# Expert weights loaded in the order of their use, the tail's copies and branch ahead of its choices, and two pairs' gate/up weights in halves

## The chip, the core and the metric

The kernel runs on one core of a Trainium2 chip. Its time is the device time of one execution in microseconds. The core has TensorE (matmuls, PE in the profile), VectorE (DVE), ScalarE (ACT), GpSimd (POOL) and SyncE (SP), each with its own queue of instructions that run in order; they wait for each other by semaphores. Sixteen DMA engines move data between HBM and the on-chip memory; in this kernel SyncE issues nearly all weight loads, GpSimd the gathers and scatters of rows.

## What is computed

One decoder layer on 512 rows of 1024 numbers in float32: a modulated norm, a mixer of gated linear attention and sparse softmax attention, an output projection, and then a mixture of 32 experts. The part that the change touches is the last:

```python
hg = jnp.einsum('td,edf->tef', ht, w_g)
hu = jnp.einsum('td,edf->tef', ht, w_u)
act = jax.nn.silu(hg) * hu * combine[..., None].astype(hg.dtype)
y = jnp.einsum('tef,efd->td', act, w_d)
...
y = hier_moe(h, ...)
x = x + gate_f * rmsnorm(y, g_post_ffn[l])
```

`combine` is nonzero for two experts of each row, the two choices. Each expert has a gate and an up matrix of 1024 x 256 and a down matrix of 256 x 1024.

## The kernel before

**Experts in pairs.** The 32 experts are worked off as 16 pairs (`NPAIR`), each expert with 64 places for rows. Pair j goes through: a gather of its 128 rows (GpSimd, L1226), their transposition (TensorE `turn_rows`, L870), the gate/up product (`gate_up_product`, L883, 32 matmuls into bank G or S0), silu and product (ScalarE L1624, VectorE L2278), a transposition of the result (`turn_act`, L900), the down product (`down_product`, L912, 16 matmuls into banks A0 and A1), two copies to `yb` (`y_left` on VectorE, L2288; `y_right` on ScalarE, L1638), and a scatter of the rows to `y_dram` (GpSimd, L1231). Pair 15 has no scatter; its rows stay in `yb` and are added at the end.

**TensorE's order.** Up to pair 13 (`OWN_DOWN`) the down product of pair j-1 follows the gate/up product of pair j; from pair 13 on a pair's own down product follows too. So the order of use of the weights is gate/up(1), down(0), gate/up(2), down(1), ..., gate/up(13), down(12), down(13), gate/up(14), down(14), gate/up(15), down(15).

**Weight loads.** A pair has 4 MB of gate/up weights (four loads of 1 MB) and 2 MB of down weights (two loads), in three sets of buffers, so pair j's loads go to set j % 3. SyncE issues them by `experts` (L1031), for pair j first the wait for the gate/up product of pair j-3 and its four loads, then the wait for the down product of pair j-3 and its two loads. Only pair 15 is different (L1065 to L1074): its gate/up weights come as eight loads of half the rows' length, and TensorE waits for the second halves (`we_last`) in the middle of the product.

**Tail.** When all scatters are stored (`y_stored`), SyncE loads `y_dram` in four tiles of 128 rows with both choices (`y_load`, L1080, into `yc`, 1 MB each). ScalarE scales the first choice (`first_choice`, L1668), VectorE adds the scaled second one (`both_choices`, L2321). TensorE multiplies pair 15's rows with a matrix that places and weights them (`last_hot`, L958); for tiles 0 and 1 VectorE adds that product (`add_last`, L2341), for tiles 2 and 3 TensorE adds the choices itself through an identity matmul (L954). Then come the sum of squares (ScalarE L1691, L1696), `root`, `scaled` (L2347, L2351), a square root (ScalarE L1698), `final` (L2365) and the output. ScalarE and VectorE have the first two choices ahead of their copies of pair 15. A branch on `n_ov`, the number of extra pairs for experts with more than 64 rows, stands in every engine's queue; the traced execution takes it with 0 extra pairs.

## Time and profile before

| | us |
|---|---|
| median of 3 runs | 798.15 |
| lowest and highest run | 796.47, 798.77 |
| profiled execution | 795.45 |
| its span, first to last instruction | 793.6 |
| TensorE busy in the span | 702.3 |
| VectorE busy in the span | 411.6 |
| ScalarE busy in the span | 287.9 |

Times of the trace are counted from the start of the span. The pairs begin at about 529 us and end at about 766 us; the rest of the span is the tail. A view of stretches gives busy times in a window; a timeline gives single instructions; the chain of waits is followed back from the last instruction, at each step to what released it, and "issue" in it is time in which an engine waited for nothing that the profile can name, as a load whose semaphore it does not resolve.

### The profile page before, as it was taken

How to read it: one execution, taken by the hardware profiler on the slowest of the kernel's cores; microseconds unless marked ns; L12 is line 12 of the kernel's file. 1: busy time of each engine (PE TensorE's matmuls, PEld its weight loads, DVE VectorE, ACT ScalarE, POOL GpSimd, SP SyncE). 2: the span in 40 equal slices, each digit the busy share in tenths (PEclk: the TensorE clock that was granted, in tenths of full speed). 3: DMA queues.
4: the chain of work that ended last, by engine and by line, in shares of the span. 5: the costliest groups of instructions: out<-in, count | busy, mean ns of one | idle time of the engine just before them, and what ended most of it. 6: DMA issues, size and time to landing. Idle time of an engine off the chain costs nothing.

```text
span 793.6 us, 9709 instructions
## 1 busy us (share of the span) xinstructions
PE 702.3 (88%) x3447; PEld 445.4 (56%) x3447; DVE 411.6 (52%) x876; ACT 287.9 (36%) x512; POOL 120.9 (15%) x148
## 2 busy tenths in 40 slices
PE   1899989898999999999999799989889868788974
PEld 0447747566776777777777688763333323333321
DVE  2386958998897666644312735654351211112128
ACT  5133254254447778532232225342121211111224
POOL 3064852210002112000000001010122111111000
PEclk9999999999997999999999999999989998999998
DMA  9989730411311030303355162798999999999962
GB/s 343 388 302 369 285 136 1 115 57 50 107 46 61 2 106 2 107 0 107 107 212 185 60 234 79 293 407 322 416 417 420 419 422 419 419 419 421 403 272 106
DMA packets 49724, 179.27 MB, mean 226 GB/s; under 512 B 9560, under 2 KB 13762, under 8 KB 35340
## 3 DMA queue, kind: packets, MB, share of 16 engines
q1 hardware_dynamic: 43732, 166.26, 53.7%
q0 software_dynamic: 4784, 8.19, 2.9%
q10 hardware_dynamic: 1160, 4.20, 1.4%
q8 instruction: 28, 0.46, 0.2%
q14 instruction: 20, 0.16, 0.1%
HBM read 174.13 MB, written 12.59 MB: 235 GB/s over the span
## 4 chain that ended last, share of the span: by engine, by line
PE 53%; DVE 17%; DMA 8%; issue 7%; ACT 4%; DVEq 0%; POOL 0%; ACTq 0%; SPq 0%; POOLq 0%; PEldq 0%
PE psA L479 9%; PE psA L481 8%; PE psA L480 8%; PE psS L883 6%; PE psA L912 6%; PE psG L883 5%; DVE mk_mem L1833 3%; DVE m L1832 3%; DMA y_dram<-sig_mem,tables 2%; DMA arena<-y_dram 1%; PE psT L870 1%; DVE arena_r L1781 1%; DMA xn_dram<-sig_mem 1%; DMA arena<-in_w_out_dram 1%; DMA kv<-xn_dram,tables 1%
## 5 line engine op out<-in xcount | busy, mean ns | idle before, releaser
L479 PE MATMUL psA<-arena_r 128*128 128x512 f32 x320 | 130.1, 406 | 4.7 <-DVE arena_r L1781 4.1
L480 PE MATMUL psA<-arena_r 128*128 128x512 f32 x320 | 125.9, 393 | 0.0
L481 PE MATMUL psA<-arena_r 128*128 128x512 f32 x320 | 125.8, 393 | 0.0
L1781 DVE TENSOR_TENSOR arena_r<-arena,arena_r 128x1024 fp32r<-128x1024 f32 (+1 forms) x37 | 60.5, 1657 | 38.5 <-ACT arena_r L1305 37.6
L479 PEld LDWEIGHTS psA<-arena_r 128*128 128x128 f32 x320 | 60.9, 190 | 25.6 <-issue 13.7
L883 PE MATMUL psS<-arena,kv 128*64 128x512 f32 x224 | 64.6, 664 | 11.1 <-issue 10.9
L481 PEld LDWEIGHTS psA<-arena_r 128*128 128x128 f32 x320 | 60.7, 190 | 13.4
L480 PEld LDWEIGHTS psA<-arena_r 128*128 128x128 f32 x320 | 61.0, 191 | 12.0 <-issue 0.2
L883 PE MATMUL psG<-arena,kv 128*64 128x512 f32 x208 | 58.2, 611 | 4.8 <-issue 4.8
L1305 ACT CAST arena_r<-arena 128x1024 fp32r<-128x1024 f32 (+1 forms) x31 | 49.8, 1629 | 20.7 <-DMA arena<-in_w_in_dram 10.1
L2278 DVE TENSOR_TENSOR sig_mem<-sig_mem,psS 128x256 f32<-128x256 f32 x8 | 4.9, 613 | 81.7 <-ACT sig_mem L1624 81.7
L883 PEld LDWEIGHTS psS<-arena,kv 128*64 128x64 f32 x224 | 21.7, 151 | 41.8 <-issue 41.3
L1231 POOL DMA_INDIRECT y_dram<-sig_mem,tables x16 | 15.9, 993 | 182.8 <-issue 115.1
L479 PE MATMUL psA<-arena_r,qs_mem_r 128*128 128x512 f32 x96 | 38.9, 405 | 4.3 <-DVEq L2024 3.5
L912 PE MATMUL psA<-qs_mem,sig_mem 128*64 128x512 f32 x80 | 39.2, 633 | 4.0 <-ACT sig_mem L1629 4.0
L2278 DVE TENSOR_TENSOR sig_mem<-sig_mem,psG 128x256 f32<-128x256 f32 x8 | 4.9, 612 | 65.6 <-ACT sig_mem L1624 65.6
L883 PEld LDWEIGHTS psG<-arena,kv 128*64 128x64 f32 x208 | 19.1, 140 | 28.2 <-issue 27.3
L480 PE MATMUL psA<-arena_r,qs_mem_r 128*128 128x512 f32 x80 | 31.7, 397 | 0.0
L471 PE MATMUL psA<-arena,kv 128*128 128x512 f32 x64 | 29.4, 623 | 1.8 <-DMA arena<-in_w_in_dram 1.8
L1450 ACT ACTIVATE qs_mem<-qs_mem,sm 128x128 f32<-128x128 f32 (+3 forms) x32 | 17.9, 560 | 29.5 <-DVE sm L1969 28.4
L1638 ACT COPY sig_mem<-psA 128x512 f32<-128x512 f32 x16 | 9.3, 584 | 52.0 <-PE psA L912 27.6
L1832 DVE MAX8 m<-mk_mem 128x8 f32<-128x256 f32 (+2 forms) x48 | 26.9, 560 | 2.2
(440 smaller groups left out, 1293.2 us busy)
## 6 DMA issues: line engine op xcount, KB each, us to landing
arena<-in_w_e_gate_dram SPq DMA_DIRECT2D x25, 1024.0 KB
arena<-in_w_e_up_dram SPq DMA_DIRECT2D x25, 1024.0 KB
arena<-in_w_in_dram SPq DMA_DIRECT2D x11, 2048.0 KB, 8.3
arena<-in_w_e_down_dram SPq DMA_DIRECT2D x12, 1024.0 KB, 15.6
qs_mem<-in_w_e_down_dram SPq DMA_DIRECT2D x10, 1024.0 KB, 19.7
arena<-in_w_ada_dram SPq DMA_DIRECT2D x4, 2048.0 KB, 17.1
qT<-in_w_ada_dram SPq DMA_DIRECT2D x6, 1024.0 KB, 5.4
gvs<-in_w_ada_dram SPq DMA_DIRECT2D x5, 1024.0 KB, 6.2
```

Of the source, the lines that this page charges most:

```text
L471: last = nc.tensor.matmul(a[:, :], hT[:, k, tt * P:(tt + 1) * P], w[:, k, :], start=(k == 0), stop=(k == KD - 1))
L479: nc.tensor.matmul(acc, lhs[0], rhs[0], start=start, stop=False)
L480: nc.tensor.matmul(acc, lhs[0], rhs[1], start=False, stop=False)
L481: return nc.tensor.matmul(acc, lhs[1], rhs[0], start=False, stop=stop)
L883: last = nc.tensor.matmul(ps[g][64 * q:64 * q + 64, :].rearrange("p (g f) -> p g f", g=2), h2g[:, b, k, 64 * q:64 * q + 64], gu, start=(k ...
L912: last = nc.tensor.matmul(ps[name][64 * q:64 * q + 64, :], actT[:, b, kf, 64 * q:64 * q + 64], down_sets[z][q][:, D * kf + 512 * n:D * kf ...
L1231: pool.indirect_dma_start(out=y_dram, out_offset=bass.IndirectOffsetOnAxis(ap=column, axis=0), in_=yb[:, b, :], in_offset=None, bounds_che ...
L1305: nc.scalar.copy(hi[:, part], src[:, part]).then_inc(hi_ready, 4 if q is None else 1)
L1450: nc.scalar.activation(prob[:, u % 2, hh, 0:n], prob[:, u % 2, hh, 0:n], ACT.Exp, bias=sm[:, hh, z:z + 1], scale=-1.0, accum_out=sm[:, hh, ...
L1781: V.tensor_tensor(lo[:, part], src[:, part], hi[:, part], ALU.subtract).then_inc(lo_ready, 4 if q is None else 1)
L1832: step(V.max(m8[:, :], work))
L1833: step(V.match_replace(work, m8[:, :], work, TAKEN))
```

## The change

It does five things.

- The issue order of the loads. Gate/up of pair 2 stands ahead of down of pair 1. From pair 3 on SyncE issues gate/up of pair j+1 and then down of pair j, for j from 3 to 12, and then down of pair 13. The waits are the same as before, load by load.
- The gate/up weights of pair 14 are loaded in halves too, as pair 15's; TensorE has a semaphore for each of the two pairs.
- On ScalarE and VectorE the copies of pair 15 and the branch come first, and all four choices behind them. The square root's table load and a first small root stand between branch and choices. SyncE reads the branch's number ahead of the y loads and issues these once.
- TensorE starts every tile's sum with pair 15's rows and adds the choices by an identity matmul for tiles 1, 2 and 3 (before: 2 and 3); VectorE adds only for tile 0. The order of VectorE's tail follows.
- Three small loads at the start share one semaphore; the wait for two of them is now for all three.

```diff
-            pe.wait_ge(ld_small, 32)
+            pe.wait_ge(ld_small, 48)
...
-                    pe.wait_ge(ld_a2, 16)
+                    pe.wait_ge(ld_small, 48)
...
-            def gate_up_product(j, b, z, loads, g, g_turn, last_pair=False):
+            def gate_up_product(j, b, z, loads, g, g_turn, half_pair=None):
...
-                    if last_pair and k == KD // 2:
-                        pe.wait_ge(we_last, 16 * 4)
+                    if half_pair is not None and k == KD // 2:
+                        pe.wait_ge(we_last[half_pair], 16 * 4)
...
-                pe.wait_ge(fss_ready, 4)
-
-            pe.wait_ge(yb_ready, NPAIR)
-            for tt in range(TT):
-                if tt >= 2:
-                    pe.wait_ge(sum_ready, (1, 3)[tt - 2])
+
+            def last_part(tt):
+
                 for half, (name, turns) in enumerate(sum_banks[tt]):
                     if name == "S1":
                         take("S1", "sum")
                     else:
-                        pe.wait_ge(bank[name].free, base[name] + turns)
-                    if tt >= 2:
-                        nc.tensor.matmul(ps[name][:, :], ident[:, :], yc[:, tt, 0, 512 * half:512 * (half + 1)], start=True, stop=False)
-                for half, (name, turns) in enumerate(sum_banks[tt]):
+                        pe.wait_ge(bank[name].free, base[name] + turns + (0 if name == "S0" else n_ov))
                     if half:
                         pe.wait_ge(yb_act, NPAIR)
-                    last = nc.tensor.matmul(ps[name][:, :], last_hot[:, tt, :], yb[:, 1, 512 * half:512 * (half + 1)], start=(tt < 2), stop=True)
+                    last = nc.tensor.matmul(ps[name][:, :], last_hot[:, tt, :], yb[:, 1, 512 * half:512 * (half + 1)], start=True, stop=(tt == 0))
+                if tt == 0:
+                    last.then_inc(sum_full, 1)
+
+            def other_part(tt):
+
+                pe.wait_ge(fss_ready, tt + 1)
+                for half, (name, _) in enumerate(sum_banks[tt]):
+                    last = nc.tensor.matmul(ps[name][:, :], ident[:, :], yc[:, tt, 0, 512 * half:512 * (half + 1)], start=False, stop=True)
                 last.then_inc(sum_full, 1)
+
+            pe.wait_ge(yb_ready, NPAIR)
+            for tt in range(3):
+                last_part(tt)
+            other_part(1)
+            last_part(3)
+            other_part(2)
+            other_part(3)
...
             sp.wait_ge(ring_out, len(items))
+            gate_up(2, 0, 4)
+            gate_up(2, 1, 5)
             down(1, 0, 2)
             down(1, 1, 3)
-            gate_up(2, 0, 4)
-            gate_up(2, 1, 5)
...
-            for j in range(3, NPAIR - 1):
-
-                experts(j % 3, 2 * j, 2 * j + 1, MOE_G[(j - 3) % 2], (j - 3) // 2 + 1, j - 2)
-            j, z = NPAIR - 1, (NPAIR - 1) % 3
...
+            pair_gate_up(3)
+            for j in range(3, OWN_DOWN):
+                pair_gate_up(j + 1)
+                pair_down(j)
+            pair_down(OWN_DOWN)
+            for j in range(NPAIR - 2, NPAIR):
+                z = j % 3
...
+                for half in range(2):
+                    part = slice(1024 * half, 1024 * (half + 1))
...
+                pair_down(j)
...
-            for b in range(2):
-                sp.wait_ge(y_stored[b], 16 * (NPAIR // 2))
-            y_load()
             sp.wait_ge(slot_ready, 2)
             n_ov = sp.value_load(ovi[0:1, NOV:NOV + 1], min_val=0, max_val=NOV // 2)
...
+            sp.wait_ge(y_stored[1], 16 * (NPAIR // 2))
+            sp.wait_ge(y_stored[0], 16 * (NPAIR // 2 + n_ov))
+            for tt in range(TT):
+                sp.dma_start(yc[:, tt, :, :], y_v[tt]).then_inc(yc_in[tt], 16)
...
-            first_choice(0, 1, fw_ready)
-            first_choice(1, 1, fw_ready)
             y_right(NPAIR - 1, 1, NPAIR // 2)
...
+            nc.scalar.activation(st[:, 44:45], st[:, 34:35], ACT.Sqrt)
+            first_choice(0)
+            first_choice(1)
+            square(0)
+            first_choice(2)
+            rooted(0)
+            first_choice(3)
+            for tt in range(1, TT):
+                square(tt)
+                rooted(tt)
...
-            both_choices(0, (fw_ready, 1), fss_ready)
             y_left(NPAIR - 1, 1, NPAIR // 2)
-            both_choices(1, (fw_ready, 2), fss_ready)
...
-            both_choices(2, (fw_late, 1), sum_ready)
+            both_choices(0)
             add_last(0)
+            both_choices(1)
             scaled(0)
-            both_choices(3, (fw_late, 2), sum_ready)
+            both_choices(2)
             root(0)
-            add_last(1)
-            scaled(1)
-            root(1)
             final(0)
-            final(1)
-            root(2)
-            scaled(2)
-            final(2)
-            root(3)
-            scaled(3)
-            final(3)
+            both_choices(3)
+            for tt in range(1, TT):
+                root(tt)
+                scaled(tt)
+                final(tt)
```

SyncE's queue, before, from the gate/up loads of pair 3 on (`arena` with gate and up: pair 3; then down of pair 3; then gate/up of pair 4):

```order
L1021 DMA arena<-in_w_e_gate_dram 128x2048
L1021 DMA arena<-in_w_e_up_dram 128x2048
L1029 DMA arena<-in_w_e_down_dram 128x2048 [waits A1_full]
L1029 DMA arena<-in_w_e_down_dram 128x2048
L1021 DMA arena<-in_w_e_gate_dram 128x2048 [waits S0_full]
L1021 DMA arena<-in_w_e_up_dram 128x2048
```

And in the changed kernel, the same place:

```order
L1032 DMA arena<-in_w_e_gate_dram 128x2048
L1032 DMA arena<-in_w_e_up_dram 128x2048
L1032 DMA arena<-in_w_e_gate_dram 128x2048 [waits S0_full]
L1032 DMA arena<-in_w_e_up_dram 128x2048
L1032 DMA arena<-in_w_e_gate_dram 128x2048
L1032 DMA arena<-in_w_e_up_dram 128x2048
L1040 DMA arena<-in_w_e_down_dram 128x2048 [waits A1_full]
L1040 DMA arena<-in_w_e_down_dram 128x2048
```

The four loads of pair 4, with their wait on S0 (pair 1's gate/up product), moved ahead of the two down loads of pair 3 with their wait on A1 (pair 0's down product).

ScalarE's queue at the end, before, from pair 15's second transposition copy to the first square; `yc_in0` to `yc_in3` are the y tiles (the body of the loop over extra pairs, which the rows contain in part, is not run):

```order
L1629 COPY sig_mem<-psO 128x256 [waits O_full]
L1668 ACTIVATE arena<-arena,rtmp_mem 128x1024 [waits actT_ready,yc_in0]
L1668 ACTIVATE arena<-arena,rtmp_mem 128x1024 [waits yc_in1]
L1638 COPY sig_mem<-psA1 128x512 [waits y_stored1,A1_full]
L1673 COMPARE_AND_BRANCH [waits yb_act]
```

```order
L1673 UNCONDITIONAL_BRANCH [waits yc_in3,yc_in2]
L1668 ACTIVATE arena<-arena,rtmp_mem 128x1024 [waits yc_in2]
L1668 ACTIVATE arena<-arena,rtmp_mem 128x1024 [waits yc_in3]
L1687 ACT_TABLE_LOAD
L1687 ACTIVATE st<-st 128x1
L1691 ACTIVATE qs_mem,st<-arena 128x1024 [waits sum_ready]
```

And in the changed kernel:

```order
L1637 COPY sig_mem<-psO 128x256 [waits O_full]
L1646 COPY sig_mem<-psA1 128x512 [waits actT_ready,y_stored1,A1_full]
L1673 COMPARE_AND_BRANCH [waits yb_act]
```

```order
L1673 UNCONDITIONAL_BRANCH
L1702 ACT_TABLE_LOAD
L1702 ACTIVATE st<-st 128x1
L1684 ACTIVATE arena<-arena,rtmp_mem 128x1024 [waits yc_in0]
L1684 ACTIVATE arena<-arena,rtmp_mem 128x1024 [waits yc_in1]
L1690 ACTIVATE qs_mem,st<-arena 128x1024 [waits sum_ready]
L1684 ACTIVATE arena<-arena,rtmp_mem 128x1024 [waits yc_in2]
```

The copy from A1 moved from behind two choices to ahead of all; the table load moved from behind the fourth choice to ahead of the first.

## Rows read from the trace of the kernel before

**Rows 1.** Stretches: us; busy us (count) PE PEld DVE ACT POOL; clock, DMA share, GB/s.

```profile
550.50:552.00 1.50, 1.50 (x10) 0.43 (x6) 1.22 (x6) 0.00 (x0) 0.00 (x0) 1.00 0.00 0
...
732.00:748.00 16.00, 15.05 (x70) 4.89 (x70) 2.75 (x6) 3.31 (x8) 1.96 (x2) 1.00 1.01 412
...
552.00:620.00 68.00, 62.42 (x300) 23.82 (x296) 26.36 (x68) 13.93 (x35) 11.16 (x11) 0.95 1.01 412
620.00:750.00 130.00, 105.90 (x470) 40.77 (x470) 21.12 (x48) 22.33 (x55) 16.13 (x16) 0.92 1.02 419
...
722.00:726.00 4.00, 3.98 (x12) 1.47 (x14) 0.00 (x0) 0.00 (x0) 0.61 (x1) 0.63 1.01 421
```

**Rows 2.** Chain of waits, pairs 2 to 13: start, us, what.

```profile
578.07 6.13 PE psA L912 x16
...
620.01 3.00 issue
623.01 8.78 PE psS L883 x32
...
636.62 2.54 issue
639.16 7.09 PE psG L883 x32
...
718.83 3.19 issue
722.02 8.78 PE psS L883 x32
...
732.05 3.58 PE psA L912 x16
```

**Rows 3.** TensorE's timeline, gate/up of pairs 14 and 15, down of 15.

```profile
740.66 0.59 PE L883 MATMUL psG<-gvs,kv 128*64 128x512 f32 x1
...
753.20 7.04 PE L883 MATMUL psS<-arena,kv 128*64 128x512 f32 x32
...
762.25 3.65 PE L912 MATMUL psA<-arena,sig_mem 128*64 128x512 f32 x16 [0.46 <-ACT sig_mem L1629]
```

**Rows 4.** SyncE's timeline, the loads down(3) and gate/up(4).

```profile
551.42 0.80 SPq L1029 DMA_DIRECT2D arena<-in_w_e_down_dram  x2
552.27 0.43 SPq L1021 DMA_DIRECT2D arena<-in_w_e_gate_dram  x1
```

**Rows 5.** TensorE's timeline, the operation after pair 1's gate/up product.

```profile
546.49 0.44 PE L900 MATMUL psO<-ident,sig_mem 128*128 128x128 f32 x2
```

**Rows 6.** SyncE's last weight issues, then DMA issues with us to landing.

```profile
736.31 2.13 SPq L1071 DMA_DIRECT2D arena<-in_w_e_up_dram  x1
738.49 3.76 SPq L1029 DMA_DIRECT2D arena<-in_w_e_down_dram  x2
arena<-in_w_e_up_dram SPq DMA_DIRECT2D x1, 512.0 KB, 18.6
arena<-in_w_e_down_dram SPq DMA_DIRECT2D x1, 1024.0 KB, 19.6
```

**Rows 7.** Chain of waits, the store of pair 14's rows.

```profile
754.83 6.32 DMA y_dram<-sig_mem,tables
```

**Rows 8.** ScalarE's timeline, the last choice and the table load.

```profile
774.63 1.15 ACT L1668 ACTIVATE arena<-arena,rtmp_mem 128x1024 f32<-128x1024 f32 x1 [1.33 <-DMA arena<-y_dram]
775.80 1.28 ACT L1687 ACT_TABLE_LOAD   x1
777.09 0.20 ACT L1687 ACTIVATE st<-st 128x1 f32<-128x1 f32 x1
```

**Rows 9.** VectorE's timeline, the copy of pair 15 and the last two finals.

```profile
769.41 0.69 DVE L2288 COPY sig_mem<-psA 128x512 f32<-128x512 f32 x1
...
786.25 1.28 DVE L2365 SCALAR_TENSOR_TENSOR qT<-arena,st,qT 128x1024 f32<-128x1024 f32 x1
...
789.36 1.41 DVE L2365 SCALAR_TENSOR_TENSOR qT<-arena,st,qT 128x512 f32<-128x512 f32 x2
```

More of the change, by code:

```diff
@@ L1087, in _ @@
             with sp.If(n_ov > 0):
-                sp.wait_ge(fss_ready, 2)
-                for tt in (2, 3):
-                    sp.wait_ge(yc_in[tt], 16)
                 with sp.Fori(0, n_ov) as v:
@@ L1663, in _ @@
                     act_taken(j, j % 2)
-            def first_choice(tt, loads, done):
-                act.wait_ge(yc_in[tt], 16 * loads)
-                nc.scalar.activation(yc[:, tt, 0, :], yc[:, tt, 0, :], ACT.Copy, scale=rt[:, 9, tt:tt + 1]).then_inc(done, 1)
-            first_choice(0, 1, fw_ready)
-            first_choice(1, 1, fw_ready)
             y_right(NPAIR - 1, 1, NPAIR // 2)
@@ new lines, in first_choice, with square @@
+            def first_choice(tt):
+                act.wait_ge(yc_in[tt], 16)
+                nc.scalar.activation(yc[:, tt, 0, :], yc[:, tt, 0, :], ACT.Copy, scale=rt[:, 9, tt:tt + 1]).then_inc(fw_ready, 1)
+            def square(tt):
+                if tt == 0:
+                    act.wait_ge(sum_ready, 1)
+                    nc.scalar.activation(scratch2, yc[:, tt, 0, :], ACT.Square, accum_out=st[:, tt:tt + 1]).then_inc(fms_ready, 1)
+                    return
+                act.wait_ge(sum_full, tt + 1)
+                for half, (name, _) in enumerate(sum_banks[tt]):
+                    n = tt + 20 * half
+                    nc.scalar.activation(scratch2[:, 512 * half:512 * (half + 1)], ps[name][:, :], ACT.Square, accum_out=st[:, n:n + 1]).then_inc(fms_ready, 1)
@@ L2330, in _, with both_choices @@
                     y_left(NPAIR + v, 0, NPAIR // 2 + v)
-                for tt in range(2):
-                    both_choices(tt, (fw_ready, tt + 3), fss_ready)
-                dve.wait_ge(fss_ready, 4)
-            dve.wait_ge(fss_ready, 2)
+            def both_choices(tt):
+                y = yc[:, tt, :, :]
+                dve.wait_ge(fw_ready, tt + 1)
+                V.scalar_tensor_tensor(y[:, 0, :], y[:, 1, :], rt[:, 10, tt:tt + 1], y[:, 0, :], ALU.mult, ALU.add).then_inc(fss_ready, 1)
             def add_last(tt):
+                dve.wait_ge(fss_ready, tt + 1)
                 dve.wait_ge(sum_full, tt + 1)
@@ L2353, in root @@
             def root(tt):
[L2355 to L2356 removed]
+                dve.wait_ge(fms_ready, 2 * tt + 1)
+                if tt:
                     step(V.tensor_tensor(st[:, tt:tt + 1], st[:, tt:tt + 1], st[:, 20 + tt:21 + tt], ALU.add))
```

69 lines of the change are left out of this document (22 added, 47 removed).

## The prediction

> **What bounds the kernel now.** I read the execution by stretches first. From 620 to 750 us the DMA engines are busy at a share of 1.02 while TensorE is busy for 106 of 130 us [rows 1]: the expert weights set the pace. Then I read the chain of waits [rows 2]. In each pair TensorE computes gate/up (L883), turns rows, computes the down product of the pair before (L912), and waits: 3.00 us ahead of pair 7's gate/up, 2.54 ahead of pair 8's, and so on, seven times, the last 3.19 ahead of pair 13's. Those are weights landing; gate/up products are then 16.5 us apart ((722.02 - 623.01) / 6). From 722.02 on the chain is work and handoffs only: pair 14's gate/up starts at 740.66, 18.6 us later, pair 15's at 753.20, another 12.5 us later, and its down product ends at 765.9 (762.25 + 3.65) [rows 3]. So the end is set by when pair 13's gate/up weights land and then by the tail: store of pair 14's rows, loads of y, sums, output.
>
> **Part 1, the order of the weight loads.** Before, SyncE issues down(j), then gate/up(j+1), each behind a wait for its buffers. From pair 3 on the new order is gate/up(j+1), then down(j), up to down(12); from down(13) on everything keeps its place in the stream, since down(13) stood ahead of gate/up(14) already. Two effects.
>
> (a) A hole. Pair 4's gate/up goes out at 552.27, behind down(3), which waited until 551.42 for a down product [rows 4]. Its own condition, the end of pair 1's gate/up, was fulfilled at 546.5, when TensorE's next operation starts [rows 5]. In the new order it goes out there, while the engines are still busy. From 550.5 to 552 no engine moves anything, and from 552 to 620 none rests (share 1.01) [rows 1]. So every later landing gains between 1.5 us (the stretch in which even the slowest engine was idle) and 4.7 us (551.4 - 546.7). A weight has landed when its slowest engine is done, so I go near the lower end: **2.2 us**.
>
> (b) Position. Gate/up(j+1) no longer has the 2 MB of down(j) ahead of it, a third of a pair's 6 MB: it lands 16.5 / 3 = 5.5 us earlier, for pairs 4 to 13. Pair 13's lands at 722.0 - 5.5 - 2.2 = 714.3. Down(12) lands 5.5 us behind it, at 719.8. Its product starts 10.0 us after gate/up(13) (732.05 - 722.02 [rows 2]), at 724.3, so 4.5 us of cover remain for the load that was moved back.
>
> From 714.3 TensorE keeps its distances: gate/up(14) at 732.9, gate/up(15) at 745.5. Are their weights there? The last piece of pair 15's gate/up lands at 754.9 (736.31 + 18.6), the last down piece at 760.2 (about 740.6, the second issue of the pair of rows at 738.49, + 19.6) [rows 6]. Between 722.0 and 754.9 lie down(13), gate/up(14), down(14) and gate/up(15), 12 MB, so 2.7 us per MB. With 2.2 us taken off: gate/up(14) first half 730.8, second 736.3; gate/up(15) first half 747.2, second 752.7; last down 758.0.
>
> **Part 2, halves for pair 14.** Whole, gate/up(14) would wait until 736.3; in halves its first half runs from 732.9 to 736.4: worth 3.4 us there, of which little is left behind it, because gate/up(15) waits for its own weights in either case. SyncE issues eight transfers instead of four; with the ring full an issue takes as long as the drain (2.13 us for 512 KB [rows 6]), so the split itself is hidden. Does a 512 KB transfer cost more per byte? While pair 15's halves run (732 to 748) the stream moves 412 GB/s, against 419 over the stage [rows 1]. The last down piece, a whole 1 MB, lands 5.3 us behind the last half piece: this slow rate at the end belongs to the slowest engine and not to the size. I take nothing; the ends are 0 and 5.3 - 2.7 = 2.6 us per MB.
>
> The Trainium skill (DMA: Bandwidth & Descriptors, section Bandwidth) speaks against halves: it asks for at least 1 MiB per DMA, and its section Anatomy of one DMA fits about 2 us of fixed cost to each. By that, four more transfers would cost up to 8 us of stream; the 412 GB/s say that in a full queue the fixed part overlaps.
>
> **The end of the products.** Gate/up(15) starts with its first half at 747.2, is through it at 750.7 (half of 7.0 [rows 3]), waits until 752.7 and needs 3.5 us more at the full clock. But gate/up took 8.78 us after waits of 3.0 us and more, with a granted clock of 0.63 in its first 4 us, against 7.09 after a wait of 2.54 [rows 1, 2]; here two waits of 1.7 and 2.0 us come close together. I add 1.7. End: 757.9 instead of 760.2. Down(15) starts 2.0 us later as before (762.25 against 753.20 + 7.04), at 759.9, behind its weights (758.0), and ends at **763.5, 2.4 us earlier**. That, and not 7.7, is what remains of part 1: the 5.5 us of position end with pair 13, since the last bytes keep their place.
>
> **Part 3, the tail.** Before, pair 14's rows are issued at 754.83 and stored 6.3 us later [rows 7]; then y is loaded, and the last of its four tiles is used at 774.63 [rows 8]. VectorE has its copy of pair 15 done only at 770.1 (769.41 + 0.69) [rows 9], though the product ended at 765.9: the first two choices stood ahead of it. After: the store goes out 7.7 us earlier, at 747.1, beside full traffic; with 6.3 to 11 us it ends before or at 758.0, when the weights do. The four loads queue behind those: 4 MB at 412 GB/s, the last lands at about 768.5.
>
> ScalarE: copy of pair 15 done at 764.5 (0.3 + 0.7); the branch, not seen alone, between 0 and 0.7 us, the nearest being the 0.7 between VectorE's copy end and its next choice, which contains a wait: I take 0.2. The table load and the small root (1.28 + 0.20), which stood at 775.80 behind all choices [rows 8], now stand ahead of them: 766.2. The first choice takes 1.15 [rows 8]. VectorE starts at 767.4. An operation over 1024 columns takes 1.28 us, one in two halves 1.41 [rows 9]: choice(0) 1.28, add_last(0) 1.41, choice(1), scaled(0), choice(2) 3.84, root 0.15, final(0) 1.43 with its reciprocal, choice(3) 1.28: 776.8, and 0.2 for waits on ScalarE, whose squares and choices fit between. Then three tiles at 3.1 us (789.36 - 786.25 [rows 9]), the last only to its first half: 777.0 + 3.1 + 3.1 + 2.5 = **785.7, against 790.1** (789.36 + 0.75). TensorE's identity products of tiles 1 to 3 have a choice each as cover. The small load that now shares a semaphore stands directly behind the two others; nothing.
>
> The Trainium skill (ScalarE: Activation LUTs, section What ACT_TABLE_LOAD costs) puts about 1.38 us of drain beside a load of 1.28. The row agrees in the 1.28, but the next operation starts 0.01 us behind the load [rows 8]. By the Trainium skill the gain would be up to 1.4 us smaller.
>
> **Sum.** 2.4 us by the products, 2.0 by the tail's order (24.2 us from product to last final become 22.2): 4.4. Span 793.6 - 4.4 = 789.2, profiled execution 795.45 - 4.4 = 791.1. That execution is 2.7 us under the median of the runs (798.15), so I forecast 793.7.
>
> **Rivals.** *More (0.17):* the stream gains 3.5 us or more, or the clock stays up through the short waits of gate/up(15), as it did after 2.54 us. Then down(15) ends near 761: 6 to 8 us in all, 791.3. *Only the tail (0.18):* the slowest engine gains nothing from the hole, or the stores of pairs 13 and 14 now take their share inside the stream; down(15) stays near 765.5. 796.0, at the edge of what can be told. *Nothing (0.09):* the waits inside gate/up(15) leave TensorE at 1.2 GHz to the end: its second half takes 7.0 instead of 3.5 us and down(15) 6.1 as at 578.07 [rows 2], so it ends at 767.9 and the tail's 2.0 pays for it: 798. Against it: in the chain a slow gate/up is followed by a down product of 3.58 us. *Slower (0.05):* halves cost. At the 5.3 us per MB of the last piece, pair 14's 4 MB land 10.4 us later, with all that follows: 804. Half that price, 5.2 us, gives 799; it decides from 4.4 us on, where the gain is used up. Against it: the 412 GB/s. By the rule of the Trainium skill on DMA size, 8 us, it would be 801.7.
>
> **Chances.** About 0.3% (2.4 us) is what a measurement can tell from no change. Forecast 0.51, all faster; More 0.17, faster; Only the tail 0.18, half of it faster; Nothing 0.09; Slower 0.05, of which 0.01 within the bound. Faster 0.77, same 0.19, slower 0.04. The range goes down to 789.5, into More, and up to 797.3, across Only the tail and the near side of Nothing.
>
> **What would show it.** Right: pair 4's gate/up issued at about 547 and no hole behind it; gate/up(7) without a wait; gate/up(13) at about 714; pair 15's copies ahead of all choices; the last final near 785.7. Wrong: gate/up(13) at 719 or later (a), down products waiting for their weights (b), halves of pair 14 landing more than 3 us per MB apart (part 2), a y tile landing after 772 or a pause around the table load (part 3).

## The result, and the profile after

The changed kernel takes 790.91 us, median of six runs (788.68 to 791.67). The kernel before, beside it, took 795.61 (793.08 to 798.77, six runs; the 798.15 that I started from was the median of three of these). The ratio of the two is 0.9916, 95% interval [0.9895, 0.9937]: 6.7 us (5.0 to 8.4) gained where I had forecast 4.4. The two medians as they stand differ by less, 4.7 us: the six runs of before lie in two groups, 796.5 to 798.8 and 793.1 to 794.8. I go by the ratio, since the same kernel timed again (after_again, below) gives 0.9918 with medians of 790.37 and 797.04, 6.7 us apart.

The profiled execution took 791.03 us with a span of 789.2, which is the predicted span to the tenth. That agreement is an accident, as the next paragraphs show.

Stretches of after (us; busy us and count of PE, PEld, DVE, ACT, POOL; granted clock, DMA share, GB/s), then SyncE's timeline there:

```profile
549.00:552.00 3.00, 3.00 (x20) 1.67 (x21) 2.24 (x6) 2.18 (x6) 0.00 (x0) 1.00 0.99 370
552.00:620.00 68.00, 63.25 (x306) 24.26 (x302) 27.65 (x74) 13.95 (x35) 11.17 (x11) 0.95 1.01 419
620.00:750.00 130.00, 108.45 (x498) 41.01 (x496) 22.78 (x50) 24.21 (x59) 17.10 (x17) 0.95 1.02 417
```

```profile
548.93 0.33 SPq L1032 DMA_DIRECT2D arena<-in_w_e_gate_dram  x1
...
553.77 0.81 SPq L1040 DMA_DIRECT2D arena<-in_w_e_down_dram  x2
```

Against [rows 1]: where no engine moved anything in the last 1.5 us before 552, the share is now 0.99. Pair 4's gate/up is issued at 548.93 (546.8 when its stage is set to start with that of before), ahead of down(3), and not at 552.27 behind it [rows 4]. The stage as a whole moves 419 and 417 GB/s in the two long stretches, where before moved 412, with the hole at its start, and 419.

TensorE's timeline of after at gate/up(7), gate/up(13), both halves of gate/up(15), and down(15) (start, us, what, number of matmuls, idle time before it and what ended it; of the products of pairs 7 and 13 only the first few matmuls stand in the row):

```profile
621.69 1.89 PE L884 MATMUL psS<-arena,kv 128*64 128x512 f32 x8
...
715.75 1.08 PE L884 MATMUL psS<-arena,kv 128*64 128x512 f32 x4 [2.05 <-issue]
...
749.07 3.65 PE L884 MATMUL psS<-arena,kv 128*64 128x512 f32 x16 [1.45 <-issue]
754.46 3.65 PE L884 MATMUL psS<-arena,kv 128*64 128x512 f32 x16 [1.74 <-DMA arena<-in_w_e_up_dram]
759.22 0.44 PE L901 MATMUL psO<-ident,sig_mem 128*128 128x128 f32 x2 [1.11 <-DVE sig_mem L2291]
760.21 3.65 PE L913 MATMUL psA<-arena,sig_mem 128*64 128x512 f32 x16 [0.56 <-ACT sig_mem L1637]
```

Gate/up(7) starts without the 3.00 us of wait of [rows 2]. Pair 15 is bound by its weights: the second half starts as they land, after 1.74 us.

**A common zero.** The expert stage does not start at the same time in each execution. The first gate/up product (pair 0's) starts at 529.55 in the profile of before and at 531.71 in that of after, 2.2 us later, and the one edit ahead of it does not explain this (behind the small loads with the shared semaphore, SyncE issues a load of `w_in` at 173.98 us before and 173.67 after, so they are not it). In the profiles of the kernels below it lies between 527.9 and 538.0. A good part of this goes with TensorE's granted clock far ahead of the stage: from 250 to 300 us it is 0.86 in four of the fourteen profiles, this one of after among them, and 0.93 to 0.97 in the ten others, before with 0.95. A copy of GpSimd that starts at 300.10 in before starts at 303.9 to 305.6 in those four and at 298.4 to 303.6 in the others. What makes the clock differ there no run shows. So all times of the stage are from here on counted from that product's start. In these terms the product of down(15) ends at 236.35 before (765.9 - 529.55) and 232.15 after (763.86 - 531.71), **4.2 us earlier, and not 2.4**. From there to the start of the last final it takes 23.46 us before and 21.48 after (785.34 - 763.86): **2.0 less, as forecast**. The way from there to the end of the span is 0.4 shorter (4.24 and 3.86). Sum 6.6, well inside the ratio's 5.0 to 8.4; the span shows only 4.4 of it because its stage began 2.2 late.

The tail as the chain of waits of after has it (start, us, what):

```profile
735.79 18.53 DMA arena<-in_w_e_up_dram
754.46 3.67 PE psS L884 x16
760.21 3.67 PE psA L913 x16
765.08 1.28 ACT L1702
766.58 1.05 ACT arena L1684
767.65 1.30 DVE arena L2340
...
785.34 0.75 DVE qT L2372
```

The store of pair 14 [rows 7] and the loads of y (10.04 us from 762.09 in the chain of before) are gone from it; the last piece of pair 15's gate/up weights (issued 735.79, landed 754.3), both products, then ScalarE's table load and first choice set the end.

### The profile page after: what moved, and what is told of

The parts are those of the page before. It is cut to its first block, busy times and chain, and to the rows that moved or that the text cites. A ratio compares the mean times of both kernels' runs of the same rounds, so it can differ in the third digit from the quotient of the medians.

```text
span 789.2 us, 9728 instructions
## 1 busy us (share of the span) xinstructions
PE 703.0 (89%) x3451; PEld 447.0 (57%) x3451; DVE 411.7 (52%) x876; ACT 287.7 (36%) x514; POOL 120.9 (15%) x148
## 4 chain that ended last, share of the span: by engine, by line
PE 48%; SPq 13%; DVE 13%; DMA 8%; ACT 4%; issue 3%; POOL 0%; DVEq 0%; ACTq 0%; POOLq 0%; PEldq 0%
PE psA L480 10%; PE psA L482 10%; PE psA L481 10%; SPq L1032 5%; SPq L1090 4%; SPq L1040 4%; PE psS L884 3%; PE psA L913 3%; DMA arena<-in_w_e_up_dram 2%; PE psG L884 2%; DVE mk_mem L1846 2%; DMA y_dram<-sig_mem,tables 2%; DVE m L1845 2%; PE psO L611 1%; PE psT L598 1%
## 5 line engine op out<-in xcount | busy, mean ns | idle before, releaser
L480 PEld LDWEIGHTS psA<-arena_r 128*128 128x128 f32 x320 | 61.5, 192 | 24.4 <-issue 12.3
L482 PEld LDWEIGHTS psA<-arena_r 128*128 128x128 f32 x320 | 61.5, 192 | 13.5
L481 PEld LDWEIGHTS psA<-arena_r 128*128 128x128 f32 x320 | 61.5, 192 | 12.2 <-issue 0.2
L884 PE MATMUL psG<-arena,kv 128*64 128x512 f32 x208 | 61.2, 642 | 7.6 <-issue 7.6
L884 PE MATMUL psS<-arena,kv 128*64 128x512 f32 x224 | 58.5, 611 | 9.8 <-issue 7.9
L884 PEld LDWEIGHTS psS<-arena,kv 128*64 128x64 f32 x224 | 20.1, 140 | 37.4 <-issue 36.9
L1411 ACT ACTIVATE sig_mem<-psA 128x512 f32<-128x512 f32 x16 | 9.6, 598 | 50.8 <-PE psA L482 50.8
```

The lines of the kernel that those rows point to most:

```text
L480: nc.tensor.matmul(acc, lhs[0], rhs[0], start=start, stop=False)
L481: nc.tensor.matmul(acc, lhs[0], rhs[1], start=False, stop=False)
L482: return nc.tensor.matmul(acc, lhs[1], rhs[0], start=False, stop=stop)
L884: last = nc.tensor.matmul(ps[g][64 * q:64 * q + 64, :].rearrange("p (g f) -> p g f", g=2), h2g[:, b, k, 64 * q:64 * q + 64], gu, start=(k ...
```

## The experiments

Each kernel was timed against the kernel before in the same rounds on the same chip, in several sets of rounds on several chips. All ratios are to before, with 95% intervals; they are not quotients of the medians, from which they differ by 0.1% at most, and by 0.25% for the changed kernel. "gate/up(13)" and "product end" count from pair 0's gate/up; tail is from product end to the start of the last final. The three come from the timelines of one profiled execution of each kernel, the ratio from 6 to 12.

| kernel | ratio, interval | gate/up(13) | product end | tail |
|---|---|---|---|---|
| before | 1 | 192.5 | 236.35 | 23.46 |
| changed kernel | 0.9916 [0.9895, 0.9937] | 184.0 | 232.15 | 21.48 |
| after_again | 0.9918 [0.9881, 0.9955] | 183.4 | 231.76 | 21.45 |
| order_only | 0.9954 [0.9933, 0.9975] | 183.3 | 232.44 | 23.26 |
| tail_only | 0.997 [0.9954, 0.9986] | 193.2 | 236.70 | 21.46 |
| whole14 | 0.9912 [0.9885, 0.994] | 183.6 | 233.06 | 21.47 |
| hole_only | 0.9963 [0.9944, 0.9981] | 189.2 | 233.06 | 23.43 |
| place_only | 0.9999 [0.9978, 1.002] | 187.4 | 235.27 | 24.02 |
| early_table | 0.9894 [0.9873, 0.9915] | 183.2 | 231.38 | 20.09 |
| halves_all | 0.9987 [0.9969, 1.0006] | 188.0 | 236.41 | 21.48 |
| thirds_table | 0.9907 [0.9887, 0.9927] | 183.1 | 234.38 | 20.08 |
| thirds_filled | 0.9929 [0.9905, 0.9954] | 183.8 | 234.47 | 20.08 |
| early_filled | 0.9915 [0.9889, 0.994] | 183.7 | 233.56 | 20.08 |
| thirds_fill2 | 0.992 [0.9893, 0.9947] | 183.7 | 232.05 | 20.06 |

### The change taken apart: order, tail, halves

**order_only** is the kernel before with only the new order of the loads; **tail_only** is the changed kernel with the old order of the loads and with pair 14's gate/up weights whole. The loads in tail_only, against the changed kernel:

```diff
+            down(1, 0, 2)
+            down(1, 1, 3)
             gate_up(2, 0, 4)
             gate_up(2, 1, 5)
-            down(1, 0, 2)
-            down(1, 1, 3)
...
-            pair_gate_up(3)
-            for j in range(3, OWN_DOWN):
-                pair_gate_up(j + 1)
+            for j in range(3, NPAIR - 1):
+                pair_gate_up(j)
                 pair_down(j)
-            pair_down(OWN_DOWN)
-            for j in range(NPAIR - 2, NPAIR):
+            for j in range(NPAIR - 1, NPAIR):
```

> The kernel before with the new order of the loads alone: gate/up(j+1) ahead of down(j), pair 2's gate/up ahead of pair 1's down. Pair 14's gate/up whole, the tail as before. Theory (landings): relative to the start of the pairs, pair 13's gate/up starts 7 to 9 us earlier, pair 15's gate/up ends about 4.3 us earlier (its second half still lands last) and its down product too. The tail's old order then works with y tiles that land some 6 us earlier, so 4 to 6 us in all, ratio 0.993 to 0.995. Rival (the tail carries the gain, the stream is bound by its bytes): pair 15's down product ends within 1 us of before, ratio 0.998 to 1.000.

> The changed kernel with the old order of the loads and pair 14 whole: only the tail is new. Theory: from the end of pair 15's down product to the last final 22.2 us instead of 24.2, all products where they were, 2.0 to 2.3 us in all, ratio 0.997 to 0.998. Rival (the tail's order is worth the greater part of the measured 6.7 us): 20 us or less from product to last final, ratio 0.993 or below.

Order alone gives 3.7 us (1 - 0.9954, of 796.7), tail alone 2.4; 0.9954 x 0.997 = 0.9924, against 0.9916 for the whole. At the product end order_only gains 3.9 us where I had 2.4 for this part, and tail_only nothing (236.70); tail_only's tail is 2.0 shorter, order_only's 0.2. order_only's 0.9954 falls just short of the 0.993 to 0.995 that I had expected for it, with 4.3 us expected at the product end.

**whole14** is the changed kernel with pair 14's gate/up weights in whole loads again:

```diff
-            for j in range(NPAIR - 2, NPAIR):
+            pair_gate_up(NPAIR - 2)
+            pair_down(NPAIR - 2)
+            for j in range(NPAIR - 1, NPAIR):
```

> The changed kernel with pair 14's gate/up loaded whole; pair 15 in halves as in both. Theory (halves of pair 14 are not on the path that ends last): gate/up(14) starts about 3 us later, gate/up(15) up to 2 us later, but its second half's landing still decides: its end and the time as in the changed kernel within 0.5 us, ratio to before 0.991 to 0.993. Rival 1 (halves are worth what they cover, 3.4 us): about 3 us slower than the changed kernel, ratio 0.995 to 0.997. Rival 2 (small transfers cost stream time): faster than the changed kernel by 2 us or more, ratio below 0.990.

0.9912 against 0.9916: halves of pair 14 are worth nothing that can be seen in time, either way. Its product end of 233.06 in the profile, 0.9 us behind the changed kernel's where at most 0.5 was expected, has another cause, of which below. The last piece of pair 15 comes earlier here: the second half of gate/up(15), which waits for it, starts at 221.7 from the start of pair 0's gate/up, against 222.75 in the changed kernel, 222.45 in after_again and 222.07 in early_table, which have pair 14 in halves.

### Hole and position apart

**hole_only**: the old order, except that gate/up(4) goes ahead of down(3). **place_only**: the new order from down(4) on, except that gate/up(4) stays behind down(3).

First hole_only against the old order, written out in the names of the changed kernel, then place_only against the new one (both keep the tail, pair 14 and the gate/up(2) of before):

```diff
             pair_gate_up(3)
+            pair_gate_up(4)
             pair_down(3)
-            pair_gate_up(4)
             pair_down(4)
```

```diff
             pair_gate_up(3)
-            for j in range(3, OWN_DOWN):
+            pair_down(3)
+            pair_gate_up(4)
+            for j in range(4, OWN_DOWN):
                 pair_gate_up(j + 1)
                 pair_down(j)
```

> The kernel before with a single move: pair 4's gate/up loads ahead of pair 3's down loads; every later load keeps its place. Theory: no stretch without DMA between 547 and 553 (relative to the start as before), every later landing 2.2 us earlier (between 1.5 and 3.5), pair 15's second half lands about 2.2 us earlier, product and tail move with it: 1.8 to 2.5 us, ratio 0.997. Rival (the slowest engine gains nothing from the hole, landings stay): ratio 0.999 to 1.001, pair 13's gate/up within 0.5 us of before.

> The kernel before with the loads of gate/up(j+1) ahead of down(j) from j = 4 on, while down(3) stays ahead of gate/up(4), so that the hole at 550.5 to 552 us stays; tail and pair 14 as before. All times here count from the start of pair 0's gate/up product. Theory (position and hole are two separate gains): pair 13's gate/up starts about 5.5 us earlier than the 192.5 of before, at 186 to 187.5, but the last half piece of pair 15 lands where it did (225.4), so the product end is set by weights at 235.4 to 236.0 against 236.35, and the time is within 0.1% of before (794.8 to 795.6 where before is 795.6). Rival (position is what pays at the end too): of the 3.9 us that the whole new order gained at the product end, position carries half or more; then the product end is at 234.4 or earlier and the time 793.6 or less, ratio 0.9975 or less.

The hole is most of it: 2.9 of the 3.7 us in time, more than the 1.8 to 2.5 expected, and 3.3 at the product end. Its size could have been read from the trace of before: the DMA share there is 0.12 from 549 to 550.5 us, 0.00 to 552 and 0.76 to 554, which makes 3.3 us of rest for the mean engine, against 0.35 in hole_only (0.89, 0.88 and 1.02). The position by itself moves gate/up(13) 5.1 us forward (192.5 - 187.4; 5.5 forecast), but its product end only 1.1, and the tail gives half of that back (24.02 against 23.46); in time nothing. That is the step of the forecast that the 5.5 us of position end with pair 13, and it holds. Neither kernel moves the loads of pair 2: at gate/up(13) hole and position give 3.3 + 5.1 = 8.4 us and order_only 9.2; what that move is worth by itself was not tested. Pair 15's second half in place_only, by TensorE's timeline:

```profile
750.92 3.60 PE L883 MATMUL psS<-arena,kv 128*64 128x512 f32 x16
755.27 3.65 PE L883 MATMUL psS<-arena,kv 128*64 128x512 f32 x16 [0.75 <-DMA arena<-in_w_e_up_dram]
```

755.27 - 529.76 (its first gate/up) = 225.5. Before, the last half piece landed at 225.4 (754.9 - 529.55): same bytes ahead, same landing. In the changed kernel it lands at 222.6 (754.3 - 531.7), so the stream gained 2.7 us, of which place_only shows that the position is not the cause.

### The size of the pieces

**halves_all** gives the gate/up weights of pairs 3 to 13 the same halves as pairs 14 and 15:

```diff
             def pair_gate_up(j):
-                next_gate_up(j % 3, 2 * j, 2 * j + 1, MOE_G[(j - 3) % 2], (j - 3) // 2 + 1)
+                z, g = j % 3, MOE_G[(j - 3) % 2]
+                sp.wait_ge(bank[g].full, moe_base[g] + (j - 3) // 2 + 1)
+                for half in range(2):
+                    part = slice(1024 * half, 1024 * (half + 1))
...
+                            sp.dma_start(gu_sets[z][q][:, 2048 * n:2048 * (n + 1)][:, part], src[2 * j + q][:, part]).then_inc(we_in[z], 16)
```

> The changed kernel with the gate/up weights of pairs 3 to 13 in pieces of 512 KB as well: 44 more transfers in the stream, same bytes, same order. Theory (in a full queue a transfer has no fixed price): the stream keeps its 417 GB/s within 1%, landings and time stay within 0.5 us (790.4 to 791.4 where the changed kernel has 790.9). Rival (each transfer has a fixed price that isn't hidden): the smallest price that could be seen, 0.05 us each, gives 2.2 us; by the Trainium skill, DMA: Bandwidth & Descriptors, which asks for at least 1 MiB per DMA and has about 2 us of fixed cost for each, 44 of them would cost up to 88 us.

The theory falls. Product end is 4.3 us later than in the changed kernel, and the ratio goes from 0.9916 to 0.9987. The DMA engines' summary from 552 to 750 us, first after, then halves_all:

```profile
DMA packets 15385, 82.69 MB, mean 418 GB/s; under 512 B 3453, under 2 KB 3453, under 8 KB 7144
```

```profile
DMA packets 20910, 81.71 MB, mean 413 GB/s; under 512 B 4069, under 2 KB 4069, under 8 KB 17819
```

And the stretches (columns as above), one of after and then those of halves_all:

```profile
540.00:550.00 10.00, 9.28 (x50) 4.58 (x50) 1.99 (x5) 2.44 (x7) 0.99 (x1) 1.00 0.96 394
```

```profile
540.00:550.00 10.00, 8.92 (x47) 4.32 (x48) 1.96 (x6) 2.84 (x8) 0.99 (x1) 1.00 0.96 303
552.00:620.00 68.00, 65.39 (x316) 25.24 (x314) 28.62 (x75) 14.59 (x37) 11.20 (x11) 0.97 1.03 413
620.00:750.00 130.00, 105.40 (x470) 39.85 (x468) 21.39 (x48) 22.66 (x57) 16.16 (x16) 0.91 1.02 412
```

The engines are no less busy (share 1.02 and 1.03), but move 0.98 MB less in the window, 2.3 us of stream, with 5,500 packets more: the shorter rows come as more and smaller packets. Another 0.9 MB (2.2 us) is missing from 540 to 550, where after moves 394 GB/s and halves_all 303. Together that is, within 0.2, the 4.3 us, or 0.1 us on average for each of the 44 transfers more. The starts of the products that wait for their weights agree: gate/up(9), with 28 transfers more ahead of it, comes 2.5 us later than in the changed kernel, gate/up(13), with all 44, 4.0. Whether the price is one per transfer or one per packet this experiment does not tell, since both rose together. My reason for costing halves at nothing, that 412 GB/s is close to 419, overlooked that a difference of this size matters once it holds for the whole stage. For pair 14 alone, four transfers, it is by this average 0.4 us, which whole14 could not resolve in time. The Trainium skill (DMA: Bandwidth & Descriptors, section Bandwidth) has the right sign with its advice of at least 1 MiB per DMA; the 2 us of fixed cost of its section Anatomy of one DMA would make 88 us of 44 transfers (an estimate from a figure that the page fits to single transfers issued by GpSimd; those here are issued by SyncE into a full queue), and the trace shows a twentieth of that.

### The table load

**early_table** moves the small root, and with it the table load, to ahead of ScalarE's copy of pair 15:

```diff
+            nc.scalar.activation(st[:, 44:45], st[:, 34:35], ACT.Sqrt)
             y_right(NPAIR - 1, 1, NPAIR // 2)
...
-            nc.scalar.activation(st[:, 44:45], st[:, 34:35], ACT.Sqrt)
             first_choice(0)
```

> The changed kernel with the load of the table for the root moved once more: from behind pair 15's copy (765.08 us, 1.28 us) to ahead of it, where ScalarE waits 3.84 us for pair 15's down product. Theory (with the order of the changed kernel, ScalarE's chain copy, branch, table, first choice sets the tail): the first choice starts 1.5 us earlier (1.28 of load, 0.20 of small root), VectorE's first combined choice too, and all behind it; tail from product end to last final 21.5 - 1.5 = 20.0, time 0.9981 of the changed kernel's, 789.4 where that has 790.9. Rival (VectorE or the loads of y set the tail, or loading the table holds the queue longer than its row shows): 0.5 us or less, tail 21.0 or more.

ScalarE's timeline of early_table:

```profile
758.00 0.37 ACT L1637 COPY sig_mem<-psO 128x256 f32<-128x256 f32 x1 [1.16 <-PE psO L901]
758.48 1.28 ACT L1672 ACT_TABLE_LOAD   x1
759.77 0.20 ACT L1672 ACTIVATE st<-st 128x1 f32<-128x1 f32 x1
762.13 0.58 ACT L1646 COPY sig_mem<-psA 128x512 f32<-128x512 f32 x1 [2.15 <-PE psA L913]
763.32 2.19 ACT L1686 ACTIVATE arena<-arena,rtmp_mem 128x1024 f32<-128x1024 f32 x2 [0.61 <-ACT sig_mem L1646]
```

The load now lies in a wait, and 2.15 us of that wait are left. The tail is 1.4 us shorter, in this profile (20.09) and in the four more that have the edit (20.06 to 20.08; without it 21.45 to 21.48 in five). That is the load of 1.28 and 0.1 for the small root, not 1.5. It gives the lowest time of the study, 788.24 us, ratio 0.9894, near what was expected (0.9981 of the changed kernel's time, with a tail of 20.0); the interval still overlaps that of the changed kernel. The Trainium skill (ScalarE: Activation LUTs, section What ACT_TABLE_LOAD costs) has about 1.38 us of drain beside the load; here the next operation starts 0.01 us behind it, and taking the load off the path brings 1.4 us and not 2.7.

### The clock at the end of the products

My sum had 1.7 us for a clock lost across the two short waits of gate/up(15). In the changed kernel it was not lost, and in none of the nine profiles of kernels with the new order and the new tail does gate/up(15) run at the lower clock, whatever its waits. Stretches of after, the wait for the second half and the second half:

```profile
752.60:754.40 1.80, 0.12 (x2) 0.00 (x0) 0.00 (x0) 0.00 (x0) 0.00 (x0) 1.00 0.76 316
754.40:758.20 3.80, 3.65 (x16) 1.27 (x16) 0.00 (x0) 0.05 (x1) 0.00 (x0) 1.00 0.34 142
```

To see whether it can be, four kernels move the wait or fill it. **thirds_table** is early_table with pair 15's second half in two quarters, the last one waited for with two of eight steps left. **thirds_filled** is thirds_table with five products more ahead of down(15), whose results nothing uses, **thirds_fill2** the same with two. **early_filled** is early_table with four of them ahead of gate/up(15)'s second half. The first two cuts are of thirds_table, the last two of thirds_filled:

```diff
+                    if half_pair == 1 and k == 6:
+                        pe.wait_ge(we_last[2], 16 * 4)
...
-                for half in range(2):
+                for half, part in enumerate((slice(0, 1024), slice(1024, 2048)) if j == NPAIR - 2 else (slice(0, 1024), slice(1024, 1536), slice(1536, 2048))):
...
+            def fill(n):
+                pe.wait_ge(bank["T0"].free, base["T0"] + NPAIR)
+                for i in range(n):
+                    nc.tensor.matmul(ps["T0"][:, :], ident[:, :], h2g[:, 1, 0:4, :], start=True, stop=True)
...
                     turn_act(j, j % 2)
+                    if j == NPAIR - 1:
+                        fill(5)
```

> The early table load together with a third piece in pair 15: its gate/up rows come as one half and two quarters, and the product waits for the last quarter with two of its eight steps left instead of four. Counted from the start of pair 0's gate/up. Theory (the last piece of gate/up sets the product end): it lands where the second half landed (222.6), behind it lie 1.8 us of gate/up instead of 3.6, but the last down weights land at 227.5 and down(15) started at 228.5, so at most 1.0 us is to be had: product end 231.2 to 231.6 instead of 232.15, tail 20.0, sum 2.1 to 2.5 us under the changed kernel: 788.6 where that has 790.9, ratio to before 0.989. Rivals: the quarters add nothing to the early table (789.4), since pair 15's first half or the rows it multiplies come too late for it; or smaller pieces land later and it is slower than the early table alone.

> The kernel of thirds_table with five products more (identity by pair 15's rows, 512 columns, into a free bank, results unused) between the turn of pair 15's activations and its down product, where TensorE waited 2.62 us for weights and then ran at a granted clock of 0.50 (6.39 us instead of 3.65). Theory (the waits around the last product can cost the clock, the mechanism of my added 1.7 us, which only did not strike in the profile of the changed kernel): kept busy, TensorE runs down(15) in 3.65 to 3.8 us, product end 231.4 to 231.9 from the start of pair 0's gate/up instead of 234.38, and the time comes down to that of early_table or 1 us under it: ratio 0.988 to 0.989. Rival (the clock fell for another reason): down(15) stays at 5 us or more, ratio stays at 0.9907. Second rival: the fill delays the product itself, start of down(15) later than 228.4.

> The kernel of early_table with four such products ahead of the second half of pair 15's gate/up, where TensorE waited 1.88 us and kept its full clock. Theory (that wait alone does not cost the clock in most executions): product end 231.3 to 231.8, time as early_table within 0.1%, ratio 0.9885 to 0.990. Rival (in the timed executions, unlike the profiled one, the clock often falls there): the fill takes 0.8 us or more off the median, ratio 0.9885 or less.

> The kernel of thirds_filled with two products instead of five ahead of down(15). In the trace each of them shows as two passes, five took 4.46 us, 0.89 each, twice what I had counted; two take 1.8 us, less than the 2.62 us of wait that they stand in. Theory (the fill keeps the clock, and only its length spoiled the time): down(15) starts at 227.9 to 228.4 from the start of pair 0's gate/up, set by its weights, takes 3.65 us, product end 231.5 to 232.1, tail 20.1: ratio 0.988 to 0.990, as early_table (0.9894), since the last down weights, not the gate/up piece, now set the end. Rival (the third piece costs time elsewhere in most executions): ratio 0.991 or more with the product end at 233 or later.

TensorE's timeline of thirds_table, and a stretch of its down product:

```profile
749.42 7.23 PE L886 MATMUL psS<-arena,kv 128*64 128x512 f32 x32
757.75 0.44 PE L903 MATMUL psO<-ident,sig_mem 128*128 128x128 f32 x2 [1.11 <-DMA arena<-in_w_e_down_dram]
760.80 6.39 PE L915 MATMUL psA<-arena,sig_mem 128*64 128x512 f32 x16 [2.62 <-issue]
```

```profile
760.00:764.00 4.00, 3.20 (x8) 1.14 (x10) 0.00 (x0) 0.20 (x1) 0.00 (x0) 0.50 0.91 338
```

The third piece does its part: gate/up(15) runs almost without a pause and ends 1.9 us earlier than in early_table (223.8 against 225.7). But down(15) can start only at 228.0, 0.3 later than there: its own weights set that. The wait has only moved: instead of 1.88 us inside gate/up and 0.46 ahead of down(15) it is 2.62 ahead of down(15), and only 0.44 of work parts it from the 1.11 before. Behind it the granted clock is 0.50, the lower level of 1.2 GHz, and the product takes 6.39 instead of 3.65 us.

With the wait filled (thirds_filled, TensorE's timeline) the clock stays:

```profile
754.36 4.46 PE L894 MATMUL psT<-kv,ident 128*128 128x512 f32 x10
758.75 3.65 PE L921 MATMUL psA<-arena,sig_mem 128*64 128x512 f32 x16
```

So down(15) takes the 3.65 us of the theory. As the loss is rare even without a fill (below), one profile of each kernel does not show that the fill is what kept the clock. The fill was too long, however: each product in float32 shows as two matmuls in the row (x10), 0.89 us together, twice what I had counted, and down(15) starts 2.8 us later, at 230.8. Two products instead of five (thirds_fill2) put it at 228.39 with 3.65 us and the product end at 232.05, where expected. The timed runs give 0.992 [0.9893, 0.9947] where 0.988 to 0.990 was expected, which neither confirms that nor excludes it. Its own profile is behind that of early_table: 0.7 us at the product end, and 0.7 behind the last final, where the span ends 4.53 us after that final's start against 3.83. All three kernels with a third piece have this (4.42 to 4.53); its cause is open.

In the timed executions the clock is probably not lost as a rule. thirds_table's profiled execution, with 6.39 us, took 793.5 us; its five others took 788.1 to 790.8. If the slow product were the rule, a median of 790.1 would be hard to explain, though with stages that start up to 10 us apart the times alone do not prove it. early_filled, which was expected to cost nothing, cost 2.2 us at the product end and 0.2% in the ratio: its four products take 3.70 us in a wait of 1.88. Of the nine profiles of kernels with the new order and the new tail, down(15) is slow in two: thirds_table, and whole14, where it took 5.26 us behind waits of 1.11 and 0.90, as this stretch shows:

```profile
757.80:763.00 5.20, 5.18 (x16) 1.58 (x16) 0.69 (x1) 0.00 (x0) 0.00 (x0) 0.68 0.84 319
```

The changed kernel's two profiles, after_again the second, show it in neither.

The length of the waits does not decide it. place_only has almost the waits of whole14 (0.75 us inside gate/up(15), then 1.11 and 0.90; whole14 0.69, 1.11 and 0.90), and its down(15) takes 3.65 us. In the same profile of place_only one gate/up product takes 7.1 us behind a wait of 3.22 and another 8.8 behind one of 2.62. And a wait between the halves of a pair can cost the clock too: in thirds_table the second half of gate/up(14) takes 5.35 us behind 1.95, where in the changed kernel it takes 3.66 behind 1.58. What else decides is not shown.

> The changed kernel itself once more, on the same chip and in the same rounds as the two filled kernels, as their yardstick and to see by how much the size of its gain changes from one set of rounds to the next. Expected: ratio 0.990 to 0.993 (the first set gave 0.9916), product end 232.0 to 233.8, tail 21.5. If my sum of 4.4 us was right and the first set was lucky, it would be 0.994 to 0.995. In its profile pair 15's gate/up either keeps a granted clock of 1.00 across its waits (9.0 us with a wait of 1.7 to 2.6 inside) or loses it (10.5 us or more).

The ratio came as expected, 0.9918 [0.9881, 0.9955]. This interval alone would not exclude my 4.4 us, a ratio of 0.9945; that of the first set, up to 0.9937, does. Product end and tail are 231.76 and 21.45, and pair 15's gate/up keeps its clock: 3.65 us for each half behind waits of 1.45 and 1.87.

## Why the forecast was right and wrong

- **The hole (1a), right in place, too small.** 2.2 us taken between 1.5 and 4.7, on the ground that a weight lands when its slowest engine is done. The last piece landed 2.7 us earlier (225.4 to 222.6), and the hole alone moves the product end by 3.3 (hole_only); the mean share of the engines, above, would have given about 3. Another 0.5 us in the changed kernel.
- **The position (1b), right.** Gate/up(13) 8.4 us earlier (7.7 forecast), of which position alone 5.1; no wait ahead of gate/up(7), nor of a down product for its weights. That this ends with pair 13 is what place_only shows: 0.9999.
- **Halves for pair 14, right in size, wrong in reason.** Nothing to be seen (0.9912 without them). But a half is not free: halves_all shows 0.1 us for each further transfer, 0.4 for pair 14. The price of *Slower*, 5.3 us per MB, is a misreading: between the last half piece and the last down piece lie both down loads of pair 15, 2 MB [rows 6], so it is 2.7 us per MB, the plain rate of the stream.
- **"I add 1.7", the step that failed.** I took a clock loss as certain across waits of 1.7 and 2.0 us, though the same chain showed gate/up at 7.09 us after a wait of 2.54 [rows 2]. The waits were 1.45 and 1.74 us here, both halves took 3.65 us, and the clock stayed at 1.00 in both profiles of the kernel: the term measured nothing. Such a loss does strike now and then (5.35 us for half a product behind 1.95, 6.39 for down(15) behind 1.11 and 2.62, both in thirds_table). That the clock stays up was a rival with its own chance (the second condition of *More*); the loss belonged there and not in the sum.
- **The tail, right.** 2.0 us forecast, 1.98 measured, 2.0 in tail_only too. The branch took 0.6 us instead of 0.2, and the single steps between made up for it.
- **The end of the span** came 0.4 us earlier behind the last final; I had not looked for it. It goes with the new tail (3.80 to 3.88 us in seven profiles with it, 4.19 to 4.25 in four without), except in the three kernels with a third piece.
- **The sum and the base.** 4.4 + 1.7 + 0.5 = 6.6, the measured sum; the 0.4 at the end of the span is used up by handoffs in pair 15 that I had a few tenths short. From the median of three runs that I had, the ratio gives 791.4 (798.15 x 0.9916), against 793.7 forecast and 790.91 measured; the half us between 791.4 and 790.9 is less than runs of one kernel differ by. That the predicted span came true to the tenth is luck: 2.2 us too little gain and a stage that began 2.2 us late.

The rivals: *Only the tail* and *Nothing* fall with the product end at 232.15, *Slower* with whole14. *More* is what happened, in its size (6 to 8 us) and by its second condition, the clock. Its first, a stream that gains 3.5 us or more, did not come true: it gained 2.7.

What stays open: what decides whether a short wait costs the clock, whether early_table is faster than the changed kernel in time (its tail is), whether the third piece with a fill of the right length adds anything, and why the granted clock ahead of the stage, and with it the stage's start, differs from one execution to the next.

## What to carry to other kernels

A load that waits in its queue behind a wait of another load costs its hole once for the whole stream behind it; reordering that stops the hole is worth more than a reordering that lets loads land earlier while the last bytes keep their place. Take a term that is known to strike only sometimes as a rival and not into the sum. When the last weights set the end, look at which load is next late before cutting the one that is late now: the third piece gained 1.9 us in one product and lost all of it at the next. And set a common zero ahead of the part under study before comparing two profiles.

## What the runs showed of the hardware

- Ahead of the part that was changed, executions differ by more than most edits of this study are worth: pair 0's gate/up starts at 527.9 us in one profile and at 538.0 in another, and a copy at 300 us already at 298.4 and 305.6, with a granted clock of 0.97 and 0.86 from 250 to 300. Comparing spans of single profiles misled by 2.2 us here.
- With 1 MB transfers split into halves of their rows, 418 GB/s become 413 at a busy share that is no lower (1.01 and 1.02 from 552 to 750), 0.1 us for each transfer more.
- A load of ScalarE's table (1.28 us) that was put into a wait cost nothing that shows: 2.15 us of the wait were left. The operation behind it follows after 0.01 us.
- Behind two waits with 0.44 us of work between them, 3.7 us together, the granted clock was 0.50 for the 6.4 us of product in one profile; in two profiles with the second wait filled the product took its 3.65 us. Waits of 0.7, 1.11 and 0.90 us gave 5.26 us in one profile and 3.65 in another.
